# Two attentions of a two-block kernel: scores of two heads as adjacent 64-row matmuls, two units a step

## The reference

```
h = rms_norm(x, g_mix_pre)
q_f, k_f, v_f, f_logit, q_c, k_c, v_c = split(h @ w_in)
# "fox": causal, with a decay c = cumsum(log_sigmoid(f_logit + b_fgate)) per head
s = q_f.k_f / sqrt(64) + c_t - c_s,   s <= t
# "chunked": chunks of 64 tokens; a chunk sees itself and the 8 chunks before it,
# which at 512 tokens is every earlier chunk
s = q_c.k_c / sqrt(64) + rel_bias[head, clipped distance]
o = softmax(s) @ v
```

## Time and profile before

| | |
|---|---|
| device time, median of 3 | 1649.55 us (1648.57 to 1652.32) |
| span of the profiled execution (no other time of it is given) | 1645.6 us |
| FOX, first score load to the first of CHUNKED | 167.10 to 223.90 us |
| CHUNKED, to the first matmul of the next projection | 223.90 to 278.98 us |
| TensorE busy | 1583.7 us, 96% of the span |
| VectorE busy | 885.4 us, 54% |
| ScalarE busy | 586.6 us, 36% |
| mean granted TensorE clock | 0.983 of 2.4 GHz |

### The profile page before, as it was taken

The page is one execution under the profiler, slowest core; times in us unless marked ns, Lnnn a source line. Parts: engine busy times, 40 slices in busy tenths (PEclk is TensorE's granted clock), DMA queues, the critical chain, the costliest instruction groups (busy, mean ns, idle before and its releaser), DMA issues.

```text
span 1645.6 us, 22730 instructions
## 1 busy us (share of the span) xinstructions
PE 1583.7 (96%) x8177; PEld 1325.4 (81%) x8177; DVE 885.4 (54%) x1180; ACT 586.6 (36%) x790; POOL 187.1 (11%) x95
## 2 busy tenths in 40 slices
PE   6999999998998999999998999999999999999998
PEld 4889777986886888888886687878998788888887
DVE  6223776536545534433333865466886766666333
ACT  6322433643244322222224423233434433333322
POOL 0010001024004100000003443432000200000000
PEclk9999999998998999999998999999999999999999
DMA  5433000522112233333222032221001233333331
GB/s 158 134 123 103 1 1 26 179 87 68 51 52 77 77 102 93 86 101 103 102 86 93 26 102 78 79 100 51 1 0 51 77 102 94 86 101 103 102 102 52
DMA packets 159965, 132.05 MB, mean 80 GB/s; under 512 B 6300, under 2 KB 151964, under 8 KB 159908
## 3 DMA queue, kind: packets, MB, share of 16 engines
q1 hardware_dynamic: 158004, 128.11, 25.3%
q0 software_dynamic: 848, 3.17, 0.6%
q10 hardware_dynamic: 1056, 0.00, 0.0%
HBM read 129.15 MB, written 2.12 MB: 80 GB/s over the span
## 4 chain that ended last, share of the span: by engine, by line
PE 90%; DVE 5%; ACT 1%; issue 1%; POOL 1%; DMA 0%; DVEq 0%; ACTq 0%; SPq 0%; POOLq 0%
PE ps L1473 25%; PE ps L1475 24%; PE ps L1474 24%; PE ps L1678 5%; PE ps L1666 2%; PE ps L414 2%; POOL x_t L701 1%; PE ps L1764 1%; DVE work L1074 1%; PE ps L447 1%; PE ps L1695 1%; PE ps L1614 1%; PE ps L540 1%; DVE x_t L1111 1%; DVE work L1167 1%
## 5 line engine op out<-in xcount | busy, mean ns | idle before, releaser
L1473 PE MATMUL ps<-a_hi,w_hi 128*128 128x512 f32 (+2 forms) x1672 | 659.2, 394 | 26.3 <-DVE a_lo L1095 14.5
L1475 PE MATMUL ps<-a_hi,w_lo 128*128 128x512 f32 (+2 forms) x1672 | 647.0, 387 | 0.0
L1474 PE MATMUL ps<-a_lo,w_hi 128*128 128x512 f32 (+2 forms) x1672 | 646.9, 387 | 0.0
L1473 PEld LDWEIGHTS ps<-a_hi,w_hi 128*128 128x128 f32 (+1 forms) x1672 | 315.1, 188 | 103.9 <-issue 32.0
L1058 DVE TENSOR_TENSOR w_lo<-raw,w_hi 128x2048 fp32r<-128x2048 f32 x94 | 215.5, 2293 | 291.7 <-ACT w_hi L735 291.1
L1474 PEld LDWEIGHTS ps<-a_lo,w_hi 128*128 128x128 f32 (+1 forms) x1672 | 315.3, 189 | 66.0 <-issue 4.6
L1475 PEld LDWEIGHTS ps<-a_hi,w_lo 128*128 128x128 f32 (+1 forms) x1672 | 314.9, 188 | 65.0 <-issue 0.3
L735 ACT ACTIVATE w_hi<-raw 128x2048 fp32r<-128x2048 f32 x118 | 225.5, 1911 | 292.8 <-PE ps L1475 291.2
L1343 DVE TENSOR_TENSOR arena<-ps,rstd 128x512 f32<-128x512 f32 x88 | 60.1, 689 | 173.3 <-PE ps L1475 166.9
L706 POOL TENSOR_TENSOR w_lo<-raw,w_hi 128x2048 fp32r<-128x2048 f32 x24 | 110.2, 4591 | 320.3 <-ACT w_hi L735 320.3
L1678 PE MATMUL ps<-arena,work 128*128 (+2 forms) x768 | 110.1, 284 | 5.0 <-DVE work L1167 4.3
(11 more groups left out here) (184 smaller groups left out, 1363.4 us busy)
## 6 DMA issues: line engine op xcount, KB each, us to landing
raw<-in_w_gate_up SPq DMA_DIRECT2D x44, 512.0 KB, 4.6
raw<-in_ffn_w_up SPq DMA_DIRECT2D x44, 512.0 KB, 4.7
raw<-in_attn_w_in SPq DMA_DIRECT2D x36, 512.0 KB, 4.0
raw<-in_w_in SPq DMA_DIRECT2D x24, 512.0 KB, 4.7
raw<-in_w_down SPq DMA_DIRECT2D x22, 512.0 KB, 4.1
raw<-in_ffn_w_down SPq DMA_DIRECT2D x22, 512.0 KB, 4.1
raw<-in_w_mem_kv SPq DMA_DIRECT2D x16, 512.0 KB, 3.9
raw<-in_w_out SPq DMA_DIRECT2D x8, 512.0 KB, 4.0
```

The lines of the kernel that those rows point to most:

```text
L1473: pe.matmul(dst, s_hi, m_hi, start=start, stop=False, skip_group_check=across)
L1474: pe.matmul(dst, s_hi, m_lo, start=False, stop=False, skip_group_check=across)
L1475: return pe.matmul(dst, s_lo, m_hi, start=False, stop=stop, skip_group_check=across)
```

## The change

- The score of a head is a matmul over its own 64 rows of q and k, straight from the projected tiles. The zero-padded q, its copies on VectorE, its clearing and the wait for that are gone. The scale 0.125 is applied by ScalarE when it evicts q's projected tiles (`scaled_q_then_k`), whose chunks are now all straight code.
- The units of a pair are reordered: u = 0, 1 are the first block of both heads, u = 2, 3 the second, and so on, so two neighbouring units have the same number of keys.
- `Heads64.pipeline` replaces the shared one for these two attentions: two units a step, all 32 units straight code, without a loop. In a step it issues the leads of units t+2 and t+3, then the turns of t and t+1, then the values of t-2 and t-1.
- TensorE issues both scores of a step one after the other, then FOX's decay and mask matmuls of both (`lead_two`).
- The relative bias is read where it lies; GpSimd's copies of it and the waits for them are gone. The selectors of the next pair are written after the maximum of a pair's last unit.
- `peel` and the numbers in FOX, CHUNKED, MEMORY and DILATED follow from this; nothing else of the program changes.

```diff
@@ -397,38 +395,59 @@
         class Heads64(Units):
             def __init__(self, base, pads0, pads, q, v, out):
                 super().__init__(base, pads0, pads, 4, 64)
                 self.q, self.v, self.to = q, v, out
+            def keys(self, u):
+                return (u // 2 + 1) * 128
+            def pipeline(self, eng, lead, turn=None, values=None):
+                n = 8 * self.pairs
+                def two(f, t):
+                    if f and 0 <= t < n:
+                        f(t // 8, t % 8)
+                        f(t // 8, t % 8 + 1)
+                two(lead, 0)
+                for t in range(0, n + 2, 2):
+                    two(lead, t + 2)
+                    two(turn, t)
+                    two(values, t - 2)
             def pad(self, dve, p, half):
-                rows = slice(64 * half, 64 * half + 64)
-                dve.tensor_scalar(q_pad_1[rows, half, :], arena[rows, ds(p * S + (QK_1 + self.q * S), S)], 0.125, None,
-                                  ALU.mult).then_inc(q_padded, 1)
-                if self.pads == 2:
-                    dve.tensor_copy(sel_pad[:, half, :], sel_col[:, ds(p * 2 + half, 1)].to_broadcast([128, 128]))\
-                       .then_inc(q_padded, 1)
+                dve.tensor_copy(sel_pad[:, half, :], sel_col[:, p * 2 + half:p * 2 + half + 1].to_broadcast([128, 128]))\
+                   .then_inc(q_padded, 1)
             def score(self, pe, p, u):
-                half, i, n = u // 4, u % 4, self.keys(u)
-                last = pe.matmul(self.scores(u), q_pad_1[:, half, i * 128:(i + 1) * 128],
-                          flat(p * S + (QK_1 + (self.q + 4) * S), n), start=True, stop=self.pads == 1)
-                if self.pads == 1:
-                    return last
-                pe.matmul(self.scores(u), sel_pad[:, half, :], decay[:, 0:n], start=False, stop=False)
+                head = 64 * (u % 2)
+                rows, n = slice(head, head + 64), self.keys(u)
+                q, k = QK_1 + (self.q + p) * S + u // 2 * 128, QK_1 + (self.q + 4 + p) * S
+                return pe.matmul(self.scores(u), arena[rows, q:q + 128], arena[rows, k:k + n], start=True,
+                                 stop=self.pads == 0)
+            def decayed(self, pe, u):
+                n = self.keys(u)
+                pe.matmul(self.scores(u), sel_pad[:, u % 2, :], decay[:, 0:n], start=False, stop=False)
                 return pe.matmul(self.scores(u)[:, n - 128:n], ident_r[:, :], causal, start=False, stop=True)
-            def bias(self, u):
-                return rel_pad[:, u // 4, (3 - u % 4) * 128:S]
+            def bias(self, p, u):
+                return rel[:, 2 * p + u % 2, (3 - u // 2) * 128:S]
             def value(self, p, u, b):
-                return flat(p * 128 + (V_1 + (self.v + b) * HW + u // 4 * 64), 64)
+                at = V_1 + (self.v + b) * HW + p * 128 + u % 2 * 64
+                return arena[:, at:at + 64]
             def out(self, p, u):
-                return flat(p * 128 + (HEADS_1 + u % 4 * D + self.to + u // 4 * 64), 64)
+                at = HEADS_1 + u // 2 * D + self.to + p * 128 + u % 2 * 64
+                return arena[:, at:at + 64]
         class MemoryHeads(Units):
...
@@ -660,16 +679,6 @@
                 pool.dma_start(mem_tok[:, 2 * b:2 * b + 2, :],
                                A["mem"][0, b * 128:(b + 1) * 128, :].rearrange("p (h n) -> p h n", h=2))\
                     .then_inc(mem_loaded, 16)
-            pool.wait_ge(vec_turned, 1)
-            pool.memset(q_pad_1, 0.0).then_inc(pad_1_cleared, 1)
-            pool.wait_ge(scores_done, CREDIT + 32)
-            with pool.Fori(0, HEADS // 2) as p:
-                for half in range(2):
-                    pool.wait_ge(max_done, p * 8 + (CHUNKED.base + 4 * half - 4))
-                    pool.tensor_copy(rel_pad[:, half, :], flat(p * (2 * S) + (REL + half * S), S))\
-                        .then_inc(rel_padded, 1)
             pool.wait_ge(max_done, CREDIT + 64)
             pool.memset(masks_made, 0.0).then_inc(mask_step, 1)
             pool.wait_ge(mask_step, 1)
...
@@ -793,11 +802,18 @@
                             act.activation(squares[:, 2 * ch.o + j, :], ps[:, 2 * ch.o + j, :], ACT.Square)\
                                .then_inc(norm.sq, 1)
                         write(ch, j, ps[:, (ch.o * 2 + j) % 4, :]).then_inc(freed["act"], 1)
-                over_chunks(act, G[name], body, peel=int(bool(split_ahead)))
+                over_chunks(act, G[name], body, peel=max(peel, int(bool(split_ahead))))
             def feature_tiles(dst, first=0, tokens=S):
                 return lambda ch, j, src: act.activation(
                     arena[:, ds(ch.c * (2 * tokens) + (dst + (first + j) * tokens), tokens)], src[:, 0:tokens], ACT.Copy)
+            def scaled_q_then_k(first):
+                def write(ch, j, src):
+                    to = QK_1 + (first + 2 * ch.c + j) * S
+                    return act.activation(arena[:, to:to + S], src, ACT.Copy, scale=0.125 if ch.c < 2 else 1.0)
+                return write
             def token_tiles(dst, first):
                 return lambda ch, j, src: act.activation(
...
@@ -1146,17 +1162,19 @@
                     if units is CHUNKED:
                         dve.wait_ge(turned, n + 1 - units.deep)
-                        if u % 4 == 0:
-                            dve.wait_ge(rel_padded, p * 2 + (u // 4 + 1))
                         dve.sem_inc(bias_open, 1)
                         dve.tensor_tensor_reduce(out=units.probs(u), in0=units.scores(u),
-                                                 in1=units.bias(u), scale=-1.0, scalar=3e38, op0=ALU.add,
+                                                 in1=units.bias(p, u), scale=-1.0, scalar=3e38, op0=ALU.add,
                                                  op1=ALU.min, accum_out=neg_max[:, u % 4:u % 4 + 1])\
                            .then_inc(max_done, 1)
                         return
                     dve.tensor_reduce(neg_max[:, u % 4:u % 4 + 1], units.scores(u), axis=AX.X, op=ALU.max,
                                       negate=True).then_inc(max_done, 1)
+                    if units is FOX and u == 7 and not units.last(p):
+                        for half in range(2):
+                            pad(units, p + 1, half)
                 return f
             def turned_out(units):
...
@@ -1181,10 +1199,8 @@
                     dve.tensor_scalar(units.out(p, u), ps[:, 2 + u % 2, 0:units.width], row_recip[:, u % 4:u % 4 + 1],
                                       None, ALU.mult).then_inc(heads_done, 1)
-                    if u % 4 == 2 - units.ahead and not units.last(p):
+                    if units in (MEMORY, DILATED) and u % 4 == 2 - units.ahead and not units.last(p):
                         pad(units, p + 1, u // 4)
-                    elif u % 4 == 2 - units.ahead and units is FOX:
-                        pad(CHUNKED, 0, u // 4)
                     if units is DILATED and u % 4 == 2 and not units.last(p):
                         packed[u // 4].lo(dve, p + 1)
                 return f
...
@@ -1274,8 +1290,6 @@
                 dve.tensor_scalar(mem_tok[:, n, :], mem_tok[:, n, :], mem_rstd[:, n // 2:n // 2 + 1], None,
                                   ALU.mult).then_inc(mem_scaled, 1)
             splits("chunk_v")
-            dve.wait_ge(pad_1_cleared, 1)
-            dve.wait_ge(freed["act"], CREDIT + G["fox_qk"].freed_end)
             for half in range(2):
                 pad(FOX, 0, half)
             for f in range(KT):
...
@@ -1655,6 +1669,21 @@
                     units.score(pe, p, u).then_inc(scores_done, 1)
                 return f
+            def lead_two(units):
+                def f(p, u):
+                    if u % 2:
+                        return
+                    n = units.number(p, u + 1)
+                    if units is FOX and u == 0:
+                        pe.wait_ge(q_padded, units.padded(p, 1))
+                    pe.wait_ge(probs_done, n + 1 - units.deep)
+                    scored = [units.score(pe, p, u + half) for half in range(2)]
+                    for half in range(2):
+                        (scored[half] if units is CHUNKED else units.decayed(pe, u + half)).then_inc(scores_done, 1)
+                return f
             def turn_probs(units):
                 def f(p, u):
                     n = units.number(p, u)
...
@@ -1681,7 +1710,8 @@
                 return f
             def attention(units):
-                units.pipeline(pe, lead=lead(units), turn=turn_probs(units), values=values(units))
+                units.pipeline(pe, lead=(lead_two if units in (FOX, CHUNKED) else lead)(units),
+                               turn=turn_probs(units), values=values(units))
             for s in (scores_done, turned, values_done, dil_mean):
                 pe.sem_inc(s, CREDIT)
```

20 lines of the change are left out of this document (9 added, 11 removed).

## The result

Four executions of the changed kernel gave 1678.09 to 1683.10 us, median 1682.23; the kernel before, on the same chip, gave 1647.33 to 1652.32, median 1649.06. The ratio is 1.0196, 95% interval 1.0180 to 1.0211, so the change costs 33 us. Forecast were 1659.5 us and a range of 1647 to 1675. The direction was right, the size was not: some 23 us are missing from the sum.

The account below looks back on a forecast made before the run. The prediction took TensorE to hold FOX before the change and a closed chain of waits to bound both attentions after it. Chain 8.7 plus fill and drain 1.3 gave +10.0 us: 1655.6 span, 1659.5 median, range 1647 to 1675.

Parts of the forecast that it names:

- The chain of waits: FOX and CHUNKED: each step waits through values, copy, reciprocal, exponential and turn; 14.7 us a pair, 8.7 us more in all.
- All four links: Copy waits for values, reciprocal stands behind copy, exponential waits for reciprocal, TensorE's turn waits for exponential.
- the one link of the row sums: ScalarE's exponential of t+2 waits for VectorE's reciprocal of the unit four back; reciprocal and 0.04 to ScalarE: 0.8 us a pair.
- Fill and drain: Ends of FOX and CHUNKED: each fills and drains by two units rather than one, 0.65 us each, twice.
- The clock: Rival: TensorE waits each step in FOX and CHUNKED, so its clock falls; 4 to 15 us more, 1664 to 1675, chance 0.2.
- The likeliest case: FOX and CHUNKED bound by the waits between engines at full clock; 1655 to 1664 us, chance 0.58.
- the prediction's own signs of being wrong: Pair distance below 13.4 us, exponentials still following their maximum at once, or a low clock over whole pairs.
- The switch: TensorE changing between 64-row and 128-row matmuls, two a step, 64 in all: taken as 0, upper end 10 us.
- The overlap of scores: Only second and third score passes of a step fall together on TensorE: a quarter, at most 12 us of 49.0.
- the third rival: Scores don't fall together at all and outlast their shadow in FOX: +1 to +3 us over four pairs; no separate chance.
- What the change takes away: Loop and q copies in FOX and CHUNKED, 6.4 us, and overlapped score passes; not subtracted from the forecast.

Follow-up runs that it names:

- with fillers: Changed kernel plus 104 overwritten 512-column, 128-row matmuls ahead of the score pairs in FOX and CHUNKED: 1668.02 us, ratio 1.0114.
- with wide scores: Changed kernel with score matmuls over all 128 rows, summing both heads so the output differs: 1666.05 us, ratio 1.0105.
- the fastest version: Changed kernel with eight row sums instead of four and values issued ahead of turns, whole reference computed: 1634.95 us, ratio 0.9916.
- one program with lone narrow scores: Changed kernel with one unit a step in the order of the kernel before, straight code, 64-row scores: 1703.72, 1703.80, 1741.77 and 1748.29 us.
- turns and values one by one: Changed kernel with eight row sums and the order lead, lead, turn t, values t-1, turn t+1, values t: 1647.87 us, ratio 0.9995.

## Why the prediction was wrong

Step by step, by the prediction's own parts:

- **The chain of waits: right, and so was its price.** All four links are in the groups. 14.7 us a pair was forecast; at full clock FOX has 14.3 and 14.5 (14.59 with fillers), CHUNKED 15.01 with fillers and 14.42 with wide scores. By the fillers eight pairs cost 9.5 us instead of 8.7, and CHUNKED was slowed more than FOX, 1.56 against 0.82 us a pair, as said; in CHUNKED some of that may be the fillers'. Taking out the one link of the row sums turned the loss into a gain.
- **Fill and drain: a term mis-sized.** "0.65 us each, twice" came from a share of the chain for one unit; 7.9 us are measured in the version with fillers. The estimate took most of a unit's chain as covered by the other attention. But two units are held back, their values (16 weight loads) run with nothing beside them, and the clock is low there: 0.66 and 0.50 in the last stretches even with fillers. The last 512-key scores of the filler version come 296.99 - 282.30 = 14.7 us before the next projection, a whole pair's time, where the fastest version needs 265.83 - 256.06 = 9.8. Holding back two units isn't dear in itself: the fastest version does it too, and of its 99.6 us (166.24 to 265.83) eight pairs are 95.5, so its ends take 4.1 us, 1.1 more than before. The rest of the 7.9 comes with the order of turns before values, the low clock and the fillers' own time, and the runs don't part these.
- **The clock: the step that failed.** The likeliest case, and with it the sum, had the chain at full clock and put this term at 0. The low clock was a rival with a chance of 0.2 and 4 to 15 us on top; it happened, at the upper end of its size or beyond, and costs 14.4 us between the changed kernel and the one with fillers, and 16.2 by the one with wide scores. It is low over a whole pair (189.73 to 209.65 us), one of the prediction's own signs of being wrong. The mechanism was half right. I let it depend on waits and on thin turns and values, as at FOX's end in the earlier trace rows. The runs show that the same waits leave the clock at 1.00 in the middle of the attentions if the scores are wide, and that it can stay at 0.50 over narrow scores without waits. What the prediction should have asked is what TensorE does with the rows that it uses: the change halves them in every score. It had the sign of this in no row, since the kernel before has no 64-row matmul, and it took the overlap and the switch as the only unknowns of such a matmul.
- **The switch, taken as 0: about 0.14 us at most.** Two a step are 9 us for 64 of them, if all were on a path. Most lie in the chain's shadow, since the fillers' pairs are within 0.3 us of the forecast. The rows at the start, 8-column matmuls between transposes, didn't show it.
- **The overlap of scores, at most a quarter: in fact a half.** The assumption that only the second and third pass fall together was wrong. No gain over the kernel before comes of it, as forecast, but it does keep the scores in the chain's shadow: over 128 rows FOX's pairs take 15.0 us, 0.5 to 0.7 more, which is the 1 to 3 us over four pairs that the third rival gave for scores that don't fall together.
- **What the change takes away lies beside the chain: right.** Straight code alone is worth 3.9 us in the kernel before; in the changed one the pairs have the length of the chain without it, so nothing of it is seen. That is argued from the pairs, and no run puts the loop back.
- **The total.** 9.5 + 7.9 + 14.4 = 31.8 us is the growth of the two attentions by construction, since each term is a difference of two traces. Forecast were 8.7 + 1.3, and 0 in the likeliest case for the third. It took both the second and the third to leave the range: with the clock alone the forecast would be 1659.5 + 14.4 = 1673.9 us, and with the fillers, which take most of the low clock away, the time is 1668.02, both inside it.

Two things stay open. When exactly the clock falls isn't settled: the changed kernel has pairs at 1.00 and pairs at 0.50 with the same instructions, one program with lone narrow scores ran at 0.50 through FOX and at 1.00 through CHUNKED, and turns and values one by one kept 1.00 with narrow scores and waits. And the 14.4 us may hold some of the switch's cost, since fillers put wide matmuls in other places; that wasn't tried apart.

## What to carry to other kernels

Pairing units for the sake of one engine moves every buffer's last reader: go through each wait of the other engines and ask whether its releaser now stands a step later; here one more set of row sums, or values ahead of turns, was worth 2.5% or 2.6%. Matmuls over half the rows paid here only in adjacent pairs on different halves and with the chain of waits open, and then by 2.6 us (1634.95 against 1637.57); alone they cost more than the same matmuls over 128 rows, also at full clock (13.3 against 11.2 us for a pair of CHUNKED). Read the granted clock of each stretch before putting a price to anything that makes TensorE's work narrower or lets it wait.

## What the runs showed of the hardware that I had not expected

- Lone score matmuls over 64 of 128 rows went with a granted clock of 0.50 for about 100 us in FOX while TensorE was busy without a gap by the records, and with 1.00 in CHUNKED of the same execution: 1703.8 us against 1635.43 for the same instructions over 128 rows.
- Two float32 score matmuls on different halves of the rows overlap in full, both passes of each: 1.46 us to the next head's decay matmul against 2.30 on the same half.
- A narrow group between wide ones costs 0.28 us more than the same matmuls over 128 rows, and 0.29 by the length of a pair.
- The low clock can hold over whole pairs and go away again in a program that repeats itself: pairs of 14.3, 19.9 and 14.5 us in a row.
